# Four weight strips of a two-layer kernel get their low parts by a VectorE subtraction in place of an accumulating DMA

## The reference

```
def memory_cross_attention(h, mem_n, w_q, w_kv, w_o):
    q = (h @ w_q).reshape(b_, s_, X_HEADS, X_HEAD_DIM)
    ...
    p = jax.nn.softmax(s, axis=-1)
    o = jnp.einsum('bhsm,bmhd->bshd', p.astype(v.dtype), v).reshape(b_, s_, D_MODEL)
    return o @ w_o
...
        h = h + memory_cross_attention(rmsnorm(h, norm_x_g[l]), mem_n, w_xq[l], w_xkv[l], w_xo[l])
        u = rmsnorm(h, norm_ff_g[l]) @ w1[l]
        h = h + jnp.square(jax.nn.relu(u)) @ w2[l]
```

## Time and profile before

| | |
|---|---|
| time, median of 3 (lowest to highest) | 2029.14 us (2028.95 to 2029.5) |
| the profiled execution's own time | 2026.92 us |
| its span | 2023.8 us |
| TensorE busy | 1919.6 us, 95% |
| ScalarE busy | 1093.9 us, 54% |
| VectorE busy | 998.9 us, 49% |
| GpSimd busy | 265.2 us, 13% |
| mean TensorE clock granted | 0.977 of full |
| DMA | 345.75 MB, mean 171 GB/s |

### The profile page before, as it was taken

The page is one execution under the profiler, slowest core; times in us unless marked ns, Lnnn a source line. Parts: engine busy times, 40 slices in busy tenths (PEclk is TensorE's granted clock), DMA queues, the critical chain, the costliest instruction groups (busy, mean ns, idle before and its releaser), DMA issues.

```text
span 2023.8 us, 26516 instructions
## 1 busy us (share of the span) xinstructions
PE 1919.6 (95%) x9426; PEld 1583.0 (78%) x9426; DVE 998.9 (49%) x1622; ACT 1093.9 (54%) x1518; POOL 265.2 (13%) x310
## 2 busy tenths in 40 slices
PE   6989979998999999999999999989989989999996
PEld 4777768876888888878878788878868868888885
DVE  4176656333523132448887777577641254233134
ACT  7555465643533333454578887678564554343342
POOL 1100001110111111111111111111111101111110
PEclk9999999999999999989989999989999989999998
DMA  8744447963888888859777677857768849888884
GB/s 246 175 114 104 117 116 176 207 136 84 196 194 191 194 195 192 192 133 213 180 161 169 158 171 185 211 139 175 197 149 199 191 110 208 192 193 192 194 178 106
DMA packets 95209, 345.75 MB, mean 171 GB/s; under 512 B 10584, under 2 KB 10584, under 8 KB 94592
## 3 DMA queue, kind: packets, MB, share of 16 engines
q0 software_dynamic: 44064, 159.40, 43.6%
q1 hardware_dynamic: 46512, 169.14, 28.4%
q10 hardware_dynamic: 4528, 15.81, 2.3%
HBM read 340.04 MB, written 4.28 MB: 170 GB/s over the span
## 4 chain that ended last, share of the span: by engine, by line
PE 73%; DVE 8%; ACT 8%; DMA 6%; issue 3%; ACTq 2%; DVEq 1%; SPq 0%
PE bank L379 19%; PE bank L380 19%; PE bank L381 19%; DMA arena<-scratch 3%; DVE ssum L1939 3%; DMA wl<-in_weights 2%; PE bank L488 2%; PE bank L490 2%; PE bank L489 2%; ACT wl L917 1%; ACT wh L916 1%; ACT arena L1273 1%; PE work L457 1%; ACTq L1249 1%; PE bank L394 1%
## 5 line engine op out<-in xcount | busy, mean ns | idle before, releaser
L916 ACT ACTIVATE wh<-raw 128x1024 fp32r<-128x1024 f32 x306 | 323.4, 1057 | 637.8 <-PE bank L381 567.1
L379 PE MATMUL bank<-XAh,wh 128*128 128x512 f32 x1400 | 555.5, 397 | 24.6 <-DMA wl<-in_weights 22.6
L381 PE MATMUL bank<-XAh,wl 128*128 128x512 f32 x1400 | 547.9, 391 | 0.0
L380 PE MATMUL bank<-XAl,wh 128*128 128x512 f32 x1400 | 547.9, 391 | 0.0
L899 POOL DMA_DIRECT2D wl<-in_weights x306 | 265.0, 866 | 1726.0 <-ACT wl L917 1680.1
L379 PEld LDWEIGHTS bank<-XAh,wh 128*128 128x128 f32 x1400 | 265.0, 189 | 83.7 <-DMA wl<-in_weights 23.7
L917 ACT ACTIVATE wl<-raw 128x1024 fp32r<-128x1024 f32 x306 | 319.1, 1043 | 0.0
L381 PEld LDWEIGHTS bank<-XAh,wl 128*128 128x128 f32 x1400 | 264.7, 189 | 56.3
L380 PEld LDWEIGHTS bank<-XAl,wh 128*128 128x128 f32 x1400 | 265.3, 189 | 54.2 <-issue 0.7
L379 PE MATMUL bank<-XBh,wh 128*128 128x512 f32 x720 | 283.5, 394 | 11.4 <-DMA wl<-in_weights 11.4
L380 PE MATMUL bank<-XBl,wh 128*128 128x512 f32 x720 | 281.9, 392 | 0.0
(11 more groups left out here) (329 smaller groups left out, 2104.2 us busy)
## 6 DMA issues: line engine op xcount, KB each, us to landing
raw<-in_weights SPq DMA_DIRECT2D x298, 512.0 KB, 5.5
wl<-in_weights POOLq DMA_DIRECT2D x298, 512.0 KB, 8.0
arena<-scratch ACTq DMA_DIRECT2D x20, 512.0 KB, 8.0
wraw<-in_weights SPq DMA_DIRECT2D x8, 512.0 KB, 7.1
raw<-in_weights SPq DMA_DIRECT2D x8, 384.0 KB, 4.2
wl<-in_weights POOLq DMA_DIRECT2D x8, 384.0 KB, 6.3
h<-in_xT SPq DMA_DIRECT2D x2, 1024.0 KB, 6.4
spill<-cst ACTq DMA_DIRECT2D x8, 256.0 KB, 6.1
```

Source lines behind the costliest of these rows:

```text
L379: mm(bank[s][:, 0:w], hi, tile(X[0], k, w), start=(n == 0), stop=False)
L380: mm(bank[s][:, 0:w], hi, tile(X[1], k, w), start=False, stop=False)
L381: last = mm(bank[s][:, 0:w], lo, tile(X[0], k, w), start=False, stop=(n == len(kts) - 1))
L916: act_(wh[j % 4][:, :], raw[a % 2][:, :], ACT.Copy)
```

## The change

Two things. First, for strips xo+4 to xo+7 (`LOCAL`) ScalarE only rounds; VectorE subtracts `wl = raw - wh` from the raw buffer itself, at a place in its order behind `residual(0)` to `residual(3)`. GpSimd issues nothing for them. Second, the one count `w_neg` becomes two, `raw_free[0]` and `raw_free[1]`, one for each raw buffer, since two engines now release raw buffers; SyncE and GpSimd wait on these.

```diff
+LOCAL = [AT["xo"] + n for n in range(4, 8)]
+SUBBED = sorted(DIRECT + LOCAL)
...
-                if j in DIRECT:
-                    pe.wait_ge(w_sub, DIRECT.index(j) + 1)
+                if j in SUBBED:
+                    pe.wait_ge(w_sub, SUBBED.index(j) + 1)
...
                 a = staged_before(j)
-                sp.wait_ge(w_neg, a - 1)
+                if a > 1:
+                    sp.wait_ge(raw_free[a % 2], a // 2)
...
-                    sp.wait_ge(w_neg, i * 2 + (a + u - 1))
+                    sp.wait_ge(raw_free[u], i + a // 2)
...
-                pool.wait_ge(w_neg, staged_before(j) + 1)
+                a = staged_before(j)
+                pool.wait_ge(raw_free[a % 2], a // 2 + 1)
...
             for j in range(NS):
-                if j not in DIRECT:
+                if j not in SUBBED:
                     low(j)
...
                 act.wait_ge(raw_ready[a % 2], val(16 * (a // 2 + 1), i, 8 * per))
+                if j in LOCAL:
+                    act_(wh[j % 4][:, :], raw[a % 2][:, :], ACT.Copy).then_inc(w_rounded, 1)
+                    return
                 act_(wh[j % 4][:, :], raw[a % 2][:, :], ACT.Copy)
-                act_(wl[j % 4][:, :], raw[a % 2][:, :], ACT.Copy, scale=-1.0).then_inc(w_neg, 1)
+                act_(wl[j % 4][:, :], raw[a % 2][:, :], ACT.Copy, scale=-1.0).then_inc(raw_free[a % 2], 1)
...
+            def sub_local(j):
+
+                if j in LOCAL:
+                    a = staged_before(j)
+                    dve.wait_ge(w_rounded, SUBBED.index(j) + 1)
+                    TTop(wl[j % 4][:, :], raw[a % 2][:, :], wh[j % 4][:, :].bitcast(F32), ALU.subtract).then_inc(w_sub, 1)
+                    dve.drain().then_inc(raw_free[a % 2], 1)
...
             for n in range(KT):
                 residual(n, "xo", AT["xo"] + n, "ff_g")
+                sub_local(AT["xo"] + n + 4 if n < 4 else 0)
             invert(NORM["xo"], rstd)
```

More of the change, by code:

```diff
@@ L175, in lows @@
 def lows(j):
-    return sum(n % 4 == j % 4 for n in range(j + 1) if n not in DIRECT)
+    return sum(n % 4 == j % 4 for n in range(j + 1) if n not in SUBBED)
 def direct_turn(j):
@@ L313, in block_kernel @@
         raw_ready = [sem(f"raw_ready{s}") for s in range(NRAW)]
-        w_neg, strip_done = sem("w_neg"), sem("strip_done")
+        raw_free, strip_done = [sem(f"raw_free{s}") for s in range(NRAW)], sem("strip_done")
         w_lo = [sem(f"w_lo{s}") for s in range(4)]
@@ L1442, in sub_direct @@
                 if j in DIRECT:
-                    dve.wait_ge(w_rounded, DIRECT.index(j) + 1)
+                    dve.wait_ge(w_rounded, SUBBED.index(j) + 1)
                     TTop(wl[j % 4][:, :], wraw[j % 4][:, :], wh[j % 4][:, :].bitcast(F32), ALU.subtract).then_inc(w_sub, 1)
+            def sub_local(j):
+                if j in LOCAL:
+                    a = staged_before(j)
+                    dve.wait_ge(w_rounded, SUBBED.index(j) + 1)
+                    TTop(wl[j % 4][:, :], raw[a % 2][:, :], wh[j % 4][:, :].bitcast(F32), ALU.subtract).then_inc(w_sub, 1)
+                    dve.drain().then_inc(raw_free[a % 2], 1)
             def split(src, X, k, w=S):
```

## The result

| | before | changed |
|---|---|---|
| median, of the first comparison | 2029.05 us (4 runs, 2026.27 to 2029.5) | 2015.3 us (4 runs, 2012.26 to 2018.43) |
| ratio, with 95% interval | | 0.9942 (0.9922 to 0.9961) |
| profiled execution, its own time | 2026.92 us | 2018.43 us |
| its span | 2023.8 us | 2016.3 us |
| mean TensorE clock granted | 0.977 | 0.982 |

The change makes the kernel faster, by 0.6%. From profiled execution to profiled execution it is 8.5 us. The ratio is the record's own estimate from the runs of both kernels; it lies up to 1.4 us away from the difference of the means, here and in the experiments.

A forecast was written before the change was run, and what follows sets the result against it. TensorE, busy 95% of the span, was taken as the bound, with an 8.0 us wait ahead of xo+4. Earlier start 7.61 us plus clock 1.94 gives 9.55, so 2029.14 - 9.55 = 2019.6 us; range 2018.4 to 2023.

The forecast's parts named there:

- The start of xo+4: Ahead of xo+4, TensorE waits 0.37 us in place of 7.98; start moves from 501.70 to 494.09, gain 7.61 us.
- The clock: In xo+4, TensorE's clock stays at 1.00, so the strip takes 5.44 us in place of 7.38: 1.94 us.
- The strips behind: xo+5 to xo+7 are supplied in time; ffn1+0, the tight one, waits not at all or 0.4 us.
- The row of 3.2 us at 507.4: Old-trace load with at most one accumulation beginning; with 3.9 us elsewhere, basis for raw loads of 3.2 to 3.9 us.
- What is moved to VectorE: VectorE gains 4 x 1.22 = 4.9 us, priced at zero: fourth subtraction done (504.4) before residual 4 may start (505).
- The rule against the change: VectorE operations with two SBUF inputs might slow GpSimd's issues; no blocking seen; as rival 1.2 us, 2 in 100.
- The sum: Start of xo+4 and clock together: 7.61 + 1.94, 9.55 us gained in the stage.
- so 2029.14 - 9.55 = 2019.6: Whole kernel: the gain subtracted from the earlier median, which lies 2.2 us above the profiled execution's own time.
- -1 to +1.5: Spread around 2019.6 us, for the wake-up, the first matmul behind a wait and 0.4 us of ffn1+0.
- The range: Whole time from 2018.4 to 2023 us, taking in part of a wait moved to ffn1+0, GpSimd blocking and a clock drop.

The follow-up runs named there:

- warm_wait: The kernel before the change with 34 idle matmuls behind xo+3, filling the wait ahead of xo+4: stage 41.0 us, whole 3.5 us faster (+-2.3), ratio 0.998.
- double_sub: The changed kernel with each of the four subtractions done twice: stage 38.4 us, whole -5.2 us against before (+-2.4), ratio 0.9976.
- split_only: The kernel before with only the counts split and no strip subtracted by VectorE: stage 43.2 us, whole +1.0 us (+-2.0), ratio 1.0002.
- refill: The changed kernel with 40 idle matmuls behind xo+7, so everything behind starts as late as before: stage 43.1 us, whole +1.0 us (+-1.7), ratio 1.0005.

## Why the prediction was right in the stage and wrong in the number

**The start of xo+4.** Right to 0.01 us: rounding, subtraction and start stand as worked out, 2.37 us behind the end of xo+0, and the 7.61 us of this term came out as 7.61 (501.70 - 491.72 less 493.56 - 491.19).

**The clock.** It stayed at 1.00, as taken. The term was 1.94 us and measured 1.57 from start to start (7.18 to 5.61). I had counted 7.38 us to the end of xo+4's last matmul against a strip's 5.44 from start to start, which is 0.20 too much, and had forgotten that the first matmul behind even a short wait comes slower (0.34 us to the next in place of 0.227, and 0.50 long), with the next few some 0.01 us apart more than the rest, 0.17 in all. `warm_wait` shows the term at 1.74 with no wait at all.

**The strips behind.** Right: no wait ahead of xo+5, xo+6, xo+7 and ffn1+0; loads of 3.2 to 3.3 us; the subtractions within 0.4 us of their places. The row of 3.2 us at 507.4, which the forecast leaned on, was not a load by itself: the accumulation issued at 500.19 took 9.1 us, to 509.3, and the next one began at 508.2. That loads are quick with none in flight is shown by the changed kernel. Close to the edge, as said: `double_sub` shows the wait that comes when VectorE is late. In one of four traces, the first, ffn1+0 lost 0.2 us to a late low part of the activation.

**What is moved to VectorE.** Right in the result and wrong in the reason. The forecast had VectorE through with the fourth subtraction "before it may start residual 4 (505)". Residual 4 adds xo+4's sum, and xo+4 ends at 499.17 (forecast 499.5); 505 is the end of xo+5. So the subtractions of xo+6 and xo+7 do hold VectorE up: residual 4 starts at 504.26, straight behind the fourth, 5.1 us after it might have, and residual 5 at 506.52 although xo+5 ends at 504.61. Only at residual 6 is VectorE waiting for TensorE again:

```profile
506.52 0.69 DVE L1507 TENSOR_TENSOR h<-h,bank 128x512 f32<-128x512 f32 x1
...
510.25 0.69 DVE L1507 TENSOR_TENSOR h<-h,bank 128x512 f32<-128x512 f32 x1 [1.56 <-PE bank L383]
```

It costs nothing, since VectorE has caught up by residual 6, and xo+4's bank, free at 504.95, is wanted by ffn1+0 at 515.49 only.

**The rule against the change.** GpSimd's issue of 506.33 took 0.86 us and ended before VectorE's low part 5 (507.34); beside it ran residual 5, of whose two inputs one is in PSUM, and the last 0.1 us of a sum. The issue of 519.86 does lie under a low part with both inputs in SBUF, and took 0.88 us:

```profile
519.50 0.75 DVE L1479 SCALAR_TENSOR_TENSOR XAl<-h,vec,XAh 128x512 fp32r<-128x512 f32 x1 [1.63 <-ACT XAh L946]
...
519.86 0.88 POOL L903 DMA_DIRECT2D wl<-in_weights  x1 [5.56 <-issue]
```

Over the changed kernel's first trace at least 62 issues lie for 0.4 us or more under a VectorE operation with two inputs in SBUF; their median is 0.865 us, like that of the 105 beside an idle VectorE, and the longest took 1.02. The Trainium skill's rule (GPSIMD Engine Reference, Specifications) on GpSimd's shared SBUF interface shows next to no cost in this trace either.

**The sum.** 9.55 was forecast for the stage and 8.9 to 9.2 were measured in four traces: 7.61 and 1.57, less the 0.2 us of ffn1+0 in the first trace. Against before, run beside it, the whole moved by 10.3 us, to 1.5 either way, which holds both.

**The step that failed** is the one that turns the gain into a time, "so 2029.14 - 9.55 = 2019.6", with the spread "-1 to +1.5" put around it. It took the median of three runs as the level from which the gain is to be subtracted, and passed over that the profiled execution lay 2.2 us lower. The three are not typical: before itself had medians of 2024.4, 2024.3, 2023.5 and 2023.8 us in the four later comparisons and single runs from 2016.42 to 2032.24 us in one of them, and the changed kernel scatters over 14 us. The range held nothing for it, although beside the spread stands that a measurement of this kernel can tell about 4.1 us, and the text had no rival for anything outside of the stage. The first comparison, four runs against four, gives 13.1 us between the means, with 3.1 us to either side: that alone is more than the range reached below the forecast. It lies above all three later means, and its interval still holds 10.3. Three of its four runs of before are the very ones that the forecast used; against the fourth, 2026.27 us, the mean of the changed kernel is 11.0 us lower.

Why those three stood so high is not shown. Of the 95 later runs of before only 4 reach 2028.95 us, so three in a row would be rare luck if all runs scatter alike; whether they were taken under another condition the record does not tell.

**Open.** Whether some 1 us of the 10.3, beyond the stage, belongs to the change; by the ratios there is none. From the end of the feed-forward to 1010 (1021 in before), which the change leaves alone, TensorE needed 152.5 us in before, 152.4 in `split_only` and 151.9 in `refill`, and 150.8, 150.7, 150.8 and 151.7 in the four traces of the changed kernel. Windows of 28 us around the norm at the end of the feed-forward, in before and in the changed kernel:

```profile
864.00:892.00 28.00, 25.40 (x110) 21.55 (x110) 15.88 (x24) 14.29 (x22) 2.59 (x3) 0.82 0.60 132
```

```profile
855.00:883.00 28.00, 24.70 (x114) 20.67 (x114) 16.72 (x25) 14.08 (x23) 2.60 (x3) 0.88 0.61 130
```

The clock's drop there is shorter (mean 0.88 for 0.82). Since `refill` has 0.82 again, it looks as if when the rest of the program begins decides it; that the fourth trace of the changed kernel has 0.82 too speaks for chance. One strip alone, whose whole time did not follow its stage, is open as well: in both its traces the same part took 152.0 us, near before's 152.5, with two strips 150.6, which is too little to explain it. I didn't settle either.

## What to carry to other kernels

When a wait on TensorE is to go, price three things: the wait, the low clock behind it, and for each following consumer the moment when its own supply is ready; the gain ends at the first that is late, and here one, two and four strips gave 2.5 to 3.3, 4.5 and 9.0 us of the stage. A buffer that is now released by another engine brings that engine's program order into the supply chain, so walk that order with its durations. And before a saving is turned into an absolute time, ask how far executions of the same kernel scatter: three runs within 0.6 us did not tell it, and many runs of both kernels side by side did.

## What the runs showed of the hardware

- A load of 512 KB took 3.1 to 3.3 us alone and 8.2 to 8.8 us with two or three accumulating DMAs beside it; an accumulating one 5.6 to 9.1 us in the windows read around the change, and 4.8 to 10.6 over the whole trace of before.
- TensorE's clock stayed at 1.00 through idle times of 0.37, 1.68 and 1.83 us; behind 2.8 and 4.0 us it fell to 1.2 GHz when work had begun again (mean 1.00 in the wait, 0.76 in the strip after it, with two strips subtracted), and in the second trace with one strip within the 4.0 us (mean 0.79 in the wait). A strip behind a drop took 7.2 to 8.0 us, against 5.6 behind a wait without one.
- The length of a wait alone does not decide it. At 1663 in before a wait of 1.82 us, as long as one that did no harm in `double_sub`, is followed by the low clock (mean 0.59 over the next 3.45 us; the changed kernel has the same at 1656), while at 1138 in the changed kernel a wait of 2.81 us is not (1.00 over the next 5 us). So no length of wait is shown to be safe:

```profile
1663.23:1665.05 1.82, 0.00 (x0) 0.03 (x1) 1.38 (x2) 0.06 (x1) 0.00 (x0) 1.00 0.00 0
1665.05:1668.50 3.45, 3.45 (x10) 2.69 (x11) 2.41 (x4) 2.46 (x3) 0.70 (x1) 0.59 0.01 2
```

- Two executions of the same kernel differed by 10.5 us of span, nearly all in one stage in which TensorE waits for a chain of DMA, ScalarE and VectorE, while the feed-forward, bound by TensorE, took 332.29 us in every trace without idle matmuls in it.
